# Attention units placed between projections, their outputs turned, and the output projection fed unit by unit

## What is computed

```
layer 0:  h = x @ a_w_in ; gated recurrence (6 heads) + attention into 256 memory tokens (4 heads)
          x = LN(alpha * x + mixed @ w_o[0]);  x = LN(alpha * x + hier_moe(x))
layer 1:  q, qm = x @ b_w_in ; k, v = x @ w_kv_shared
          z = q k^T / 8 ;  a = exp(log_sigmoid(z) - sum of softplus(z) behind s), s < t   (12 heads of 64)
          seq = a @ v ;  mem = softmax(qm mem_k^T / 8) @ mem_v                            (4 heads of 64)
          x = LN(alpha * x + concat(seq, mem) @ w_o[1]);  x = LN(alpha * x + hier_moe(x))
layer 2:  q, k, v, f = x @ attn_w_in ; c = cumsum(log_sigmoid(f + b))
          o = softmax(q k^T / 8 + c_t - c_s, causal) @ v                                  (16 heads of 64)
          x = LN(alpha * x + o @ attn_w_out);  x = LN(alpha * x + conv_ffn(x))
          x = x + sigmoid(x @ ple_w_gate + b) * (p @ ple_w_proj)
```

## Time and profile before

| | us |
|---|---|
| median of 3 runs | 1069.25 (1068.37 to 1070.26) |
| the profiled execution | 1068.37 |
| its span in the trace | 1066.6 |
| PE busy | 999.5 (94%) |
| DVE busy | 713.6 (67%) |
| ACT busy | 544.5 (51%) |

### The profile page before, as it was taken

How to read it: one execution, slowest core, us unless ns; L and a number is a source line. 1 busy time by engine, 2 the same in 40 slices (tenths; PEclk the granted TensorE clock), 3 DMA queues, 4 the chain that set the end, 5 groups by cost and what they waited for, 6 DMA issues and landing times.

```text
span 1066.6 us, 15294 instructions
## 1 busy us (share of the span) xinstructions
PE 999.5 (94%) x6002; PEld 874.4 (82%) x6002; DVE 713.6 (67%) x839; ACT 544.5 (51%) x591; POOL 31.8 (3%) x65
## 2 busy tenths in 40 slices
PE   8999989899999999899999999999899999999968
PEld 7978978787787799677787777789787899997846
DVE  4788777689689855337789688845446765575563
ACT  4755643467577533643576676434453544454421
POOL 5000011000000000001000000000000000000010
PEclk9999999899999999999899999999989999999979
DMA  9544318299699767112399799646108555545601
GB/s 317 188 154 130 108 54 262 72 325 351 227 358 345 256 199 236 40 41 79 124 326 372 232 329 375 217 148 208 40 1 261 177 183 176 184 165 191 229 0 40
DMA packets 151700, 205.87 MB, mean 193 GB/s; under 512 B 6736, under 2 KB 122960, under 8 KB 151632
## 3 DMA queue, kind: packets, MB, share of 16 engines
q1 hardware_dynamic: 150768, 204.24, 56.9%
q10 hardware_dynamic: 864, 0.70, 0.2%
HBM read 203.86 MB, written 1.05 MB: 192 GB/s over the span
## 4 chain that ended last, share of the span: by engine, by line
PE 75%; DVE 10%; ACT 7%; issue 4%; DMA 4%; SPq 0%; POOL 0%; DVEq 0%; ACTq 0%
PE psum L590 72%; DVE w_lo L1750 4%; ACT w_hi L1325 3%; ACT arena L1325 2%; DVE xt_lo L1767 2%; ACT xt_hi L1325 1%; DMA raw<-in_w_up 1%; DMA x_res<-in_x 1%; DMA raw<-in_w_kv_shared 1%; PE psum L695 1%; DMA raw<-in_w_down 1%; PE psum L686 1%; ACT mt_hi L1325 1%; PE psum L998 1%; DVE x_res L1991 0%
## 5 line engine op out<-in xcount | busy, mean ns | idle before, releaser
L1750 DVE TENSOR_TENSOR w_lo<-raw,w_hi 128x2048 fp32r<-128x2048 f32 x184 | 418.3, 2289 | 113.6 <-ACT w_hi L1325 112.3
L1325 ACT ACTIVATE w_hi<-raw 128x2048 fp32r<-128x2048 f32 (+1 forms) x186 | 352.7, 1904 | 163.2 <-PE psum L590 125.4
L590 PE MATMUL psum<-w_hi,xt_hi 128*128 128x512 f32 (+1 forms) x496 | 199.0, 401 | 16.0 <-DVE xt_lo L1767 5.4
L590 PE MATMUL psum<-xt_hi,w_hi 128*128 128x256 f32 x704 | 200.1, 284 | 2.5 <-DVEq L2392 1.4
L590 PE MATMUL psum<-xt_hi,w_lo 128*128 128x256 f32 x704 | 199.2, 283 | 0.0
L590 PE MATMUL psum<-xt_lo,w_hi 128*128 128x256 f32 x704 | 199.2, 283 | 0.0
L590 PE MATMUL psum<-w_hi,xt_lo 128*128 128x512 f32 (+1 forms) x496 | 194.5, 392 | 0.0
L590 PE MATMUL psum<-w_lo,xt_hi 128*128 128x512 f32 (+1 forms) x496 | 194.4, 392 | 0.0
L590 PEld LDWEIGHTS psum<-xt_hi,w_hi 128*128 128x128 f32 x704 | 135.1, 192 | 3.9 <-issue 3.9
L590 PEld LDWEIGHTS psum<-xt_hi,w_lo 128*128 128x128 f32 x704 | 135.1, 192 | 0.0
L590 PEld LDWEIGHTS psum<-xt_lo,w_hi 128*128 128x128 f32 x704 | 135.1, 192 | 0.0
(11 more groups left out here) (241 smaller groups left out, 1192.0 us busy)
## 6 DMA issues: line engine op xcount, KB each, us to landing
raw<-in_w_gate SPq DMA_DIRECT2D x64, 512.0 KB, 5.0
raw<-in_w_up SPq DMA_DIRECT2D x64, 512.0 KB, 6.0
raw<-in_w_down SPq DMA_DIRECT2D x64, 512.0 KB, 5.3
raw<-in_ffn_w_up SPq DMA_DIRECT2D x44, 512.0 KB, 4.6
raw<-in_a_w_in SPq DMA_DIRECT2D x26, 512.0 KB, 6.7
raw<-in_attn_w_in SPq DMA_DIRECT2D x24, 512.0 KB, 5.5
raw<-in_ffn_w_down SPq DMA_DIRECT2D x22, 512.0 KB, 4.1
raw<-in_w_o SPq DMA_DIRECT2D x16, 512.0 KB, 4.4
```

The costliest lines, as they stand in the source:

```text
L590: return pe.matmul(o, l, r, start=start, stop=stop, skip_group_check=skip)
L1325: return act.activation(o, i, f, **kw)
L1750: return dve.tensor_tensor(w_half(h, w_lo), w_half(h, raw), w_half(h, w_hi).bitcast(F32), ALU.subtract).then_inc(lo_split, 1)
```

## The change

The seven K and Q projections of layer 1 and the eight of layer 2 no longer all precede the attention: PE does the first K and Q, and then runs ten steps. Step u holds `product(u-2)`, `scores(u)`, `middle(u-1)` and a filling: one of the remaining projections while there are any, and from then on parts of the output projection. The products have the values (64 columns) stationary and the weights moving, so that an output comes out feature-major, two heads in the two halves of the partitions of one bank. ACT and DVE round and split it straight into a chunk of `mt_hi` and `mt_lo` (`out_high`, `out_low`); the turns and set splits of `mixed` in layers 1 and 2 are gone. The division by the sum is now done on the weights, before the turn (`mem_norm`, `fox_norm`). Three PSUM places instead of four are in use; banks 0 and 1 take the fillings. The output projection goes chunk by chunk, with the rows of `w_o` loaded in the order of `O_ROWS`; all chunks for block 0, and the first two halves for block 1, are in the steps or right behind them; the last two halves for block 1 come last. Beside it: SP waits for `fox_taken` ahead of the load of `p`; ACT and DVE round and split the first half of layer 0's output projection sooner (inside the loop behind line 1975 for DVE); `norm` runs `split_block(then, 0)` ahead of `scale` for block 1; and the loop at line 2412 stops one half sooner.

```diff
-SETS = {"x": 0, "mem": 2, "O0": 4, "L0": 6, "L1": 10, "O1": 14, "L2": 16, "L3": 20, "O2": 24, "p": 26, "L4": 27, "L5": 31}
+SETS = {"x": 0, "mem": 2, "O0": 4, "L0": 6, "L1": 10, "L2": 14, "L3": 18, "p": 22, "L4": 23, "L5": 27}
+O_ROWS = {1: ((0, 1, 6, 7), (2, 3, 4, 5)), 2: ((0, 1, 2, 3), (4, 5, 6, 7))}
...
-            sp.wait_ge(tr_done, SETS["O2"] + 2)
+            sp.wait_ge(sem("fox_taken"), 8)
...
-        B_UNITS = [("S", 0), ("S", 1), ("M", 0), ("S", 2), ("S", 3), ("M", 1), ("S", 4), ("S", 5)]
-        C_UNITS = [("F", p) for p in range(8)]
-        SLOTS = 4
+            return ar(0 if layer == 0 else 6656, 4, 2, T)[:, h, :, :]
+
+
+
+        B_UNITS = [("S", 0), ("S", 1), ("M", 0), ("M", 1), ("S", 2), ("S", 3), ("S", 4), ("S", 5)]
+        B_CHUNK = [0, 1, 6, 7, 2, 3, 4, 5]
+        B_FILL = ["B_QM", "B_K1", "B_Q1", "B_K2", "B_Q2"]
+        B_NEEDS = {0: "B_Q0", 2: "B_QM", 4: "B_Q1", 6: "B_Q2"}
+        S_UNIT = [0, 1, 4, 5, 6, 7]
+        C_FILL = ["C_Q1", "C_K1", "C_Q2", "C_K2", "C_Q3", "C_K3"]
 
         def slot(u):
-            return 2 * (u % SLOTS)
+            return (4, 6, 2)[u % 3]
...
+            def project_chunks(layer, ks, b, js=(0, 1)):
+
+                taken, chunks = (sem("b_taken"), B_CHUNK) if layer == 1 else (sem("fox_taken"), list(range(KC)))
+                order = O_ROWS[layer][0] + O_ROWS[layer][1]
+                for j in js:
+                    for k in ks:
+                        half = 0 if k in O_ROWS[layer][0] else 1
+                        kk = O_ROWS[layer][half].index(k)
+                        h = AT[f"O{layer}"] + 2 * half + j
+                        pe.wait_ge(lo_split, h + 1)
+                        pe.wait_ge(taken, chunks.index(k) + 1)
+                        wh, wl = (w_half(h, w).rearrange("p (k n) -> p k n", k=4)[:, kk, :] for w in (w_hi, w_lo))
+                        ts = slice(P * b, P * b + P)
+                        for i, (x, w) in enumerate(passes(mt_hi[:, k, ts], mt_lo[:, k, ts], wh, wl)):
+                            last = mm(psum[:, 2 * b + j, :], x, w, k == order[0] and i == 0,
+                                      k == order[-1] and i == 2, skip=True)
+                        if b and kk == 3:
+                            last.then_inc(half_used, 1)
+                return last
+
+            def finish_projection(layer):
+
+                project_chunks(layer, O_ROWS[layer][1][3:], 0).then_inc(sem("o_done"), 1)
+                for j in range(2):
+                    project_chunks(layer, O_ROWS[layer][1], 1, (j,))
...
-            for name in ("B_K0", "B_Q0", "B_QM", "B_K1", "B_Q1", "B_K2", "B_Q2"):
+            for name in ("B_K0", "B_Q0"):
                 fm_half(name, xt_hi, xt_lo)
-            pe.wait_ge(drained_a, drained_by("B_V0", "a"))
-            pe.wait_ge(drained_v, drained_by("B_Q2", "v"))
...
+                if u in B_NEEDS:
+                    pe.wait_ge(drained_v, drained_by(B_NEEDS[u], "v"))
+                if u >= 3:
+                    pe.wait_ge(sem("b_taken"), u - 2)
...
+            def weighted_values(u, p, w):
+
+                for n, cols, out_cols in ((0, slice(0, T), slice(0, T)), (1, slice(T, 384), slice(P, T))):
                     for hh in range(2):
-                        mem_product(1, 2 * p + hh, slot(u) + hh)
+                        cs = slice(64 * (2 * p + hh), 64 * (2 * p + hh) + 64)
+                        last = mm(psum[64 * hh:64 * hh + 64, slot(u), out_cols], mixed[:, n, cs], w[:, hh, cols],
+                                  n == 0, n == 1, skip=True)
+                return last
...
+            def b_fill(u):
+
+                if u < len(B_FILL):
+                    fm_half(B_FILL[u], xt_hi, xt_lo)
                     return
-                pe.wait_ge(sem("sb_a"), p + 1)
-                for hh in range(2):
-                    o = psum[:, slot(u) + hh, 384:512]
-                    w = b_a[:, p % 2, hh, :]
-                    cs = slice(64 * (2 * p + hh), 64 * (2 * p + hh) + 64)
-                    mm(o[:, 0:64], w[:, 0:P], mixed[:, 0, cs], True, True)
-                    mm(o[:, 64:128], w[:, P:T], mixed[:, 0, cs], True, False)
-                    last = mm(o[:, 64:128], w[:, T:384], mixed[:, 1, cs], False, True)
-                last.then_inc(sem("sb_o"), 1)
-
-            def pipeline(n, scores, middle, product):
-
-                for u in range(3):
+                if u == 5:
+                    free("O10")
+                project_chunks(1, {5: (0, 1), 6: (6, 7), 7: (2,), 8: (3,), 9: (4,)}[u], 0)
+                if u >= 8:
+                    pe.wait_ge(sem("b_taken"), 6)
+                    project_chunks(1, O_ROWS[1][0], 1, (u - 8,))
+
+            for u in range(10):
+                if u >= 2:
+                    product(u - 2)
+                if u < 8:
                     scores(u)
-                for u in range(n):
-                    middle(u)
-                    if u:
-                        product(u - 1)
-                        if u + 2 < n:
-                            scores(u + 2)
-                product(n - 1)
-
-            pipeline(len(B_UNITS), scores, middle, product)
-            project(1, SETS["O1"])
+                if 1 <= u <= 8:
+                    middle(u - 1)
+                b_fill(u)
+            finish_projection(1)
...
-            for j in range(1, 4):
-                fm_half(f"C_Q{j}", xt_hi, xt_lo)
-                fm_half(f"C_K{j}", xt_hi, xt_lo)
-            pe.wait_ge(drained_a, drained_by("C_Q3", "a"))
-            pe.wait_ge(drained_v, drained_by("C_K3", "v"))
             pe.wait_ge(sem("c_split"), 2)
             pe.wait_ge(sem("pick_ready"), 1)
 
             def fox_scores(p):
 
-                if p >= SLOTS:
-                    pe.wait_ge(sem("fox_o_out"), p - SLOTS + 1)
+                if p % 2 == 0:
+                    pe.wait_ge(drained_a, drained_by(f"C_Q{p // 2}", "a"))
+                    pe.wait_ge(drained_v, drained_by(f"C_K{p // 2}", "v"))
+                if p >= 3:
+                    pe.wait_ge(sem("fox_taken"), p - 2)
...
+                if u < len(C_FILL):
+                    fm_half(C_FILL[u], xt_hi, xt_lo)
+                    return
+                if u == 6:
+                    free("O20")
+                project_chunks(2, {6: (0, 1, 2), 7: (3, 4), 8: (5,), 9: (6,)}[u], 0)
+                if u >= 8:
+                    pe.wait_ge(sem("fox_taken"), 6)
+                    project_chunks(2, O_ROWS[2][0], 1, (u - 8,))
+
+            for u in range(10):
+                if u >= 2:
+                    fox_out(u - 2)
+                if u < 8:
+                    fox_scores(u)
+                if 1 <= u <= 8:
+                    fox_turn(u - 1)
+                c_fill(u)
...
+            finish_projection(2)
...
+            round_to(AT["O0"] + 2)
...
+            def out_high(out, hi, u, chunk):
+
+                act.wait_ge(out, u + 1)
+                fn(mt_hi[:, chunk, :], psum[:, slot(u), 0:T], ACT.Copy).then_inc(hi, 1)
+
+            for u in range(10):
+                if u >= 2:
+                    out_high(sem("b_o"), sem("b_hi"), u - 2, B_CHUNK[u - 2])
+                if u < 8:
                     first(u)
-                for u in range(n):
-                    second(u)
-                    if u and u + 2 < n:
-                        first(u + 2)
-
-            pipeline(len(B_UNITS), first, second)
-            split_set(SETS["O1"])
-            split_set(SETS["O1"] + 1)
+                if 1 <= u <= 8:
+                    second(u - 1)
+                if u < 6:
+                    round_to(AT["B_KQ"] + 2 + u + 4 if u < 5 else AT["O1"] + 4)
...
-            for j in range(1, 4):
-                copy_unit(f"C_Q{j}", pair(c_q, j), 0, HD_SCALE)
-            round_to(AT["O2"] + 3)
+            round_to(AT["C_QK"] + 5)
...
+                if p == 1:
+                    split_to(AT["O0"] + 1)
...
-                    scale(b)
                     if b and then is not None:
                         split_block(then, 0)
+                    scale(b)
...
+            def out_low(hi, taken, u, chunk):
+
+                dve.wait_ge(hi, u + 1)
+                rest(mt_lo[:, chunk, :], psum[:, slot(u), 0:T], mt_hi[:, chunk, :]).then_inc(taken, 1)
...
+            for u in range(10):
+                if u >= 2:
+                    out_low(sem("b_hi"), sem("b_taken"), u - 2, B_CHUNK[u - 2])
+                if u < 8:
+                    maxima(u)
+                    softplus(u)
+                    if B_UNITS[u][0] == "M":
+                        for hh in range(2):
+                            mem_norm(2 * B_UNITS[u][1] + hh)
+                b_drain(u)
...
+                own.link(dve.reciprocal(total[:, c:c + 4], total[:, c:c + 4]))
                 for hh in range(2):
-                    inv = peak[:, 16 + c + 2 * hh:18 + c + 2 * hh]
-                    h = 2 * p + hh
-                    last = dve.tensor_tensor(mixed[:, :, 64 * h:64 * h + 64],
```

(45 more changed lines are left out.)

122 lines of the change are left out of this document (61 added, 61 removed).

## The result

The changed kernel takes 1050.87 us (median of 4 runs, 1048.18 to 1052.39) against 1069.24 (1068.37 to 1070.26): ratio 0.9833, 95% interval 0.981 to 0.9856. Predicted were 1050.8 us, and 1041 to 1060 as the range. The profiled execution took 1050.39 us, its span is 1048.7: 17.9 less than before, where the prediction summed 18.5.

A forecast was written before the change was run, and what follows sets the result against it. PE, three quarters of the chain of waits, was taken as the bound; layers 1, 2, 0 and the end gave 5.0 + 0.8 + 2.8 + 9.9 = 18.5 us off the profiled 1068.37: 1049.9, 1050.8 as a median, range 1041 to 1060.

The forecast's parts named there:

- The last norm: At the end: without the gate's third-half rounding and w_lo ahead of it, the norm starts when block 0 is done: -7.1 us.
- The swap: `split_block` ahead of `scale`: brings the gate 1.3 us nearer at the end; costed at nothing in the other norms.
- from here DVE rules: Layer 1, from block 0's norm: DVE's norm and two w_lo take 10.3 us, PE's block 1 takes 5.5.
- The wait for C's rows: Layer 2, before `scores(0)`: PE waits 6.1 us for `c_split`, no longer hidden by projections; the colder clock behind costs 2.4.
- Layer 2's cover: Layer 2's steps: fillings hide ACT, DVE and the splits, removing 13.7 us of waits and turns; whole layer -0.8 us.
- T': Start of DVE's norm of block 0 after the change, T before it: T - 5.7 in layer 1, T - 3.1 in layer 2.
- rival 4: Steps don't cover ACT and DVE: each of the 18 waits 1 us, and there is no change; chance 0.03.
- Layer 0: Output projection: the first w_lo moves into DVE's idle time, PE starts 2.25 us sooner; -2.8 us, bounds -2.2 and -4.1.
- Layer 1's clock: PE stands about 3.5 us before the logits; a falling clock makes logits and turns cost 1.3 us more, bounds 0 and 2.5.
- rival 1: New product's two column halves don't run side by side: 7.3 us less gain, 1058.1 us; chance 0.22.
- Rival 3: New product's loads and matmuls lose their overlap wholly, up to 3.4 us a unit: +40, 1091 us; chance 0.05.
- rival 2: The clock stays up at all four pauses: 10.5 us more gain, 1040.3 us; chance 0.14.

The follow-up runs named there:

- kernel 1: Kernel before with only the loop of weight splits at the last feed-forward's second half stopped earlier, ahead of the last norm: 1063.4 us, ratio 0.9949.
- kernel 12: Changed kernel with `scale` ahead of `split_block` again for block 1 in all norms: 1053.36 us, ratio 0.9864.
- kernel 9: Changed kernel with one of the two w_lo between the norms of blocks 0 and 1 made before `o_done`, layers 1 and 2: 1049.21 us, ratio 0.9821.
- kernel 8: Changed kernel with 24 idle matmuls put into PE's wait for the split of C's rows in layer 2: 1050.81 us, ratio 0.9833.
- kernel 10: Changed kernel with only layer 2's three later K copies (C_K1 to C_K3) ahead of the weight split queued before them: 1048.63 us, ratio 0.9806.
- kernel 4: Changed kernel with layer 2's K copies and the subtractions for C's rows put ahead of DVE's weight splits: 1043.2 us, ratio 0.976.
- kernel 7: Changed kernel with only the C_K0 copy and the rests of C's rows ahead of the weight split in layer 2: 1047.47 us, ratio 0.9802.
- kernel 11: Changed kernel with the edits of kernel 4 and kernel 9, and the feed-forward's first half loaded ahead of the `fox_taken` wait: 1036.77 us, ratio 0.9704.
- kernel 2: Kernel before with only the early rounding and splits of layer 0's output projection around the first attention's end: 1063.69 us, ratio 0.9951.
- Kernel 6: Changed kernel with every S and F product computed twice in layers 1 and 2, 14 units, M units not doubled: 1059.86 us, ratio 0.9904.
- kernel 5: Changed kernel with both matmuls of one head first in each new product, then those of the other, instead of alternating column halves: 1051.49 us, ratio 0.9844.

## Why the prediction was right, and where it was not

**Right, each by its own mechanism.** The last norm: -7.1 predicted, measured in the change and again alone (kernel 1). The swap: 1.3 at the end, nothing elsewhere that can be read (kernel 12). Layer 1: "from here DVE rules" holds; taking one w_lo of 2.25 us from between the norms moved block 1's norm by 2.2 (kernel 9). The wait for C's rows was 6.08 us for a predicted 6.1, and the clock behind it 0.50; a pause filled with idle matmuls keeps it at 1.00 (kernel 8), and the cost was 11.08 - 9.13 = 1.95 us for the 2.4 I took.

**Layer 2's cover, wrong in sign.** The prediction put T' at T - 3.1; it was 90.1 us behind the turn of the gate sums, against 88.1: T + 2.0. The step that failed is that the fillings of layer 2 hide ACT and DVE. I compared the sums, 5.5 us of work in a step of 8 to 10, and rival 4 did the same. What decides is the order: the copy that PE needs first stands third behind two instructions on two engines. The three waits are 4.3 us of the 5.1. In layer 1 there is none, because each projected unit has a step between its copy and its use (`B_NEEDS`); there PE waits 1.0 us in 99. Kernel 10 shows it for these waits, which are gone with the same work in another order, and kernel 4 with the rows' wait, 9.3 us less. "Waits of PE inside the steps above 1 us" was on the prediction's own list of what would be wrong. Behind T' the sum was too dear instead: I took 8.5 us for a cold `row_block` and it took 6.49, as the clock was 0.50 only up to 818.0 and 1.00 again from 819. With the load late by 0.87 the layer ended 0.9 us later against T' than before, where I had 2.3; so +3.7 in all is 5.1 less 1.4.

**The new SP wait, not free.** I had put that everything behind it would "land before they are needed". The first feed-forward half is issued behind it and behind `p` and three other loads, landed at 809.12, and its w_lo was late by 0.87 us. The chain of the changed kernel:

```profile
799.72 9.41 DMA raw<-in_ffn_w_up
...
816.07 6.49 PE psum L599 x24
```

That is little. It is 1.56 us in kernel 7, and the 2.51 us of kernel 9 are what kept that kernel from gaining in layer 2; in kernels 8 and 10 the clock took back more than the load. Kernel 11 has both this load and the w_lo moved, and the part of layer 2 that they touch is 3.1 us shorter than in kernel 4.

**Layer 0, too small.** -2.8 was predicted, with a bound of -4.1; it was -4.4 (kernel 2). I had PE start 2.25 us sooner, by the w_lo that goes, and started it behind both splits of `xt`; it starts behind the first, which holds the four chunks that its first 24 matmuls need, 3.2 us sooner. The rest is the clock, which didn't fall. In the changed kernel it is 162.94 - 147.84 = 15.1 us too; the -3.7 of the table counts from the start of the kernel, and the part up to the attention's end was 0.7 us longer in that trace.

**Layer 1's clock.** 1.3 us were predicted, and 1.26 were there at the logits (clock 0.50 from 488 to 492). But behind them the kernel before had a cold stretch of its own, 56 matmuls in 13.67 us against 12.06 after, and the 1.3 were gone. Ahead of the norms layer 1 gained more than predicted: block 0's norm starts at T - 6.5 and not T - 5.7. The new products (0.80 and 1.01 us for 0.85 and 1.06) are 0.4 of these 0.8 us; the rest was not separated.

```profile
488.00:492.00 4.00, 3.21 (x12) 2.95 (x13) 1.94 (x3) 1.83 (x3) 0.00 (x0) 0.50 0.00 0
```

The errors were +3.7 in layer 2, -0.9, -0.4, -0.8 and -1.5 in the four stretches ahead of it, and +0.5 at the end: that the total came within 0.6 us is luck in part, as errors of some 4 us each way cancelled.

**The product and rival 1.** 0.85 us was taken and 0.80 measured, but the reasoning was wrong. I read the row pair's 0.85 as an overlap of halves and put "one after the other" at 1.28, by 1.5 times the paired row. Kernel 6 shows 0.64 us for a repeated product, which is one column a cycle, and kernel 5 no effect of the order. So rival 1's mechanism holds, the halves one after the other, but not its price of 1.28 us. What the new product saves is, as I read it, instructions (no run separates this): the old one took 12 for its 1.38 us and an M unit's 16 for 1.83, 0.115 each with 64 columns; the new has eight. The Trainium skill, page "TensorEngine Tiling (Array Packing)", Key Properties, says that different tiles can load and multiply in parallel; here no gain from it is to be seen, and the measurement decides for this shape. Its sentence on a drain at a change of mode fits the 0.16 us that the first product costs over the second, though no run separates a drain from other costs of the switch. Rival 3 (3.4 us a unit) is out by the same rows; rival 2 (the clock stays up) holds in layer 0 alone.

**Open.** The two new edits of kernel 11 were not run apart in layer 2; 2.3 and 0.8 us are read from its trace. Nor was the 1.2 to 1.8 us wait ahead of the seventh product tried, where ACT's last rounding stands ahead of DVE's and thus of `fox_peak`.

## What to carry to other kernels

When work is interleaved to hide it, do not compare sums of busy time per step: follow, for each thing that the bound engine needs first in a step, the instructions queued ahead of it on the other engines. A consumer should come at least one step behind its producer, or the producer's copy must stand first in its queue. And fix waits of one chain together. When the rows alone came sooner, the next wait grew from 1.5 to 2.9 us and the clock fell behind it; the K copies alone gave 3.8 us and lost 2.3 to a colder clock behind them. Each alone gave a part (3.4 and 1.4 us in the traces), both gave 9.3.

## What the runs showed that I had not expected

The stretch of the expert layers scatters by itself. From layer 0's norm to the entry of layer 1, which only kernel 12's swap touches, the single traces lie between 207.3 and 211.8 us, and from layer 1's second norm to layer 2 between 216.5 (kernel 9) and 220.3 (kernel 4). That is as large as most effects here, so that a stretch tells what a median of six runs can't. Layer 2 itself repeats better: the changed kernel and kernels 5 and 12, which differ there only in an order, have 126.75, 126.74 and 126.57 us.

Whether the clock falls behind a pause of middling length varies. Ahead of the gate PE pauses 2.3 us, in the same code, in the changed kernel and in kernel 10. The 24 matmuls behind it take 7.35 us in the first, as shown in the chain at the top, with a granted clock of 0.61 in the first 3.2 us. The chain of kernel 10:

```profile
1018.58 5.76 PE psum L599 x24
```

There the clock was 1.00. In eight other kernels with that pause the 24 matmuls took 7.34 to 7.39 us. The 1.83 us ahead of the seventh product in layer 2 gave 0.50 and 0.53 in kernels 4 and 10, and 1.00 in kernel 11. Behind pauses of 2.9, 4.9 and 6.1 us it was about 0.5 each time, behind 1.3 and 1.7 us it was 1.00. So a stretch whose pause is near 2 us needs more than one trace.
